# Two of four gate tokens as a high and a low rounded product in the PEER gate stage

## The chip, the cores and the metric

The kernel runs on one core of one Trainium2 chip. The metric is the device time of one launch in microseconds (us). Of three runs of the kernel before, the median is 3161.97 us, the lowest 3159.41 us and the highest 3166.76 us. One further execution was profiled; every row below is from it.

## The reference, cut to what matters

The kernel computes one layer of a hybrid decoder on 1024 prompt tokens and 32 sample tokens, width 1024: a mixer (gated linear attention and S5) and then PEER, a layer of 16384 single-neuron experts of which each token uses 128. Only PEER matters here:

```python
def peer_ffn(h, w_query, sub_keys, expert_u, expert_v):
    ...
    gate = jax.nn.softmax(fin_s, axis=-1)
    idx = fin_i.reshape(T, PEER_HEADS * PEER_TOPK)
    ...
        act = jax.nn.gelu(jnp.einsum('tkd,td->tk', expert_u[ik], xk))
        return jnp.einsum('tk,tkd->td', gk * act, expert_v[ik])
```

An expert's number is `i * 128 + j`, with `i` and `j` from two lists of 128 keys. All arrays are float32. A float32 product on TensorE is one instruction of the program and two records in the trace; a product of two operands of the rounded type (`F32R`, float32 with the low mantissa bits rounded away, written fp32r where VectorE or ScalarE makes it) is one record.

## The kernel before, in words

704 of the tokens are treated densely: for them the kernel computes the activations of all 16384 experts, and multiplies them with a dense matrix of gates that is zero where a token doesn't use the expert. The other 352 tokens fetch rows of single experts by indirect DMA.

The gates stage (`peer_gates`) builds that matrix of gates. For each token it needs a 128x128 matrix W[j, i] that holds the token's 128 gates at their places. It is a product over the 128 selections: `hot_j` (selection x j, one where the selection's j is this one) is the stationary operand, `hot_i` (selection x i, the selection's gate where its i is this one, else zero) the moving one. Tokens go in groups of four (`BT`), 176 groups (`BANKS`). For each group VectorE makes `hot_j` in one instruction of 512 elements (L2478) and `hot_i` in four of 128 (L2483, `one_hots`), TensorE makes four float32 products of 128 columns into one PSUM bank (L2525), and ScalarE copies the bank out (L2546) to a buffer of 64 tokens, which SyncE writes to memory (`w_d`) when it is full.

The stage runs through 192 steps (`STEPS`), three for each of the last 64 of the 128 expert blocks. Beside the groups, each engine does its part of the expert activations (`Up`): TensorE makes in step kind 0 the first and in kind 2 the second half of a block's activations (L1894, 24 products of 352 columns of the rounded type each), in kind 1 it turns the next rows of `peer_u` (L1884, 8 transposes). ScalarE applies gelu (L1909) in kinds 0 and 2, and rounds the turned rows (L1902) in kind 1; VectorE makes the low part of them (L1914). VectorE also does the row work of the 352 sparse tokens (L1948, L1956) on rows that GpSimd fetches (L1941). Each step has then one group (two in two of the steps), as `groups_at` says. The order on each engine is the order in which the code is written; semaphores connect them:

- `hot` counts groups made by VectorE; TensorE waits for it before a group. `made` counts groups of TensorE; VectorE keeps at most three groups (`NHB`) ahead by it, and ScalarE waits for it before a copy.
- `stored` counts ScalarE's copies; TensorE waits before group g for the copy of group g - 2.
- gelu waits until the DMA of the same half of the previous block (`kept`) has landed. Those DMAs, the loads of `peer_u` and the writes of `w_d` share SyncE's queue.

## Time and profile before

| | us |
|---|---|
| median of three runs | 3161.97 |
| lowest, highest | 3159.41, 3166.76 |
| profiled execution, its own time | 3162.19 |
| its span, first to last instruction | 3160.5 |
| granted TensorE clock over the span | 0.988 |
| the gates stage, first to last group | 656.6 |

In the rows, PE is TensorE's matmul side, PEld its loads of the stationary operand, DVE VectorE, ACT ScalarE, POOL GpSimd, SP SyncE. The type of an operand of TensorE is printed as f32 whether it is float32 or rounded. A group's row gives the busy time of all its instructions together and the mean duration of one; on TensorE these durations overlap, so that the distance from one start to the next is shorter than a duration. The number after a bar is the idle time of the engine just before these instructions, and what ended it.

### The profile page before, as it was taken

How to read it: one execution, taken by the hardware profiler on the slowest of the kernel's cores; microseconds unless marked ns; L12 is line 12 of the kernel's file. 1: busy time of each engine (PE TensorE's matmuls, PEld its weight loads, DVE VectorE, ACT ScalarE, POOL GpSimd, SP SyncE). 2: the span in 40 equal slices, each digit the busy share in tenths (PEclk: the TensorE clock that was granted, in tenths of full speed). 3: DMA queues.
4: the chain of work that ended last, by engine and by line, in shares of the span. 5: the costliest groups of instructions: out<-in, count | busy, mean ns of one | idle time of the engine just before them, and what ended most of it. 6: DMA issues, size and time to landing. Idle time of an engine off the chain costs nothing. (4 is left out here: it accounts for less than half of the span.)

```text
span 3160.5 us, 45816 instructions
## 1 busy us (share of the span) xinstructions
PE 3098.8 (98%) x17420; PEld 2727.1 (86%) x17420; DVE 2510.0 (79%) x5568; ACT 882.8 (28%) x1308; POOL 929.2 (29%) x758
## 2 busy tenths in 40 slices
PE   8999989989999999999999999998999999999999
PEld 7867765489999999999999999997888888888887
DVE  6621244366889999998999999976999999999997
ACT  4210210132122222223444444432222222222222
POOL 0000000000022323323334334333554544444451
PEclk9999989989999999999999999999999999999999
DMA  3010021261167777777998898999999999999994
GB/s 105 15 42 29 14 87 47 78 190 52 54 219 243 248 243 245 246 244 239 322 349 307 330 347 309 328 339 360 357 352 336 335 351 331 336 352 340 333 339 158
DMA packets 359906, 754.88 MB, mean 239 GB/s; under 512 B 37084, under 2 KB 205880, under 8 KB 354040
## 3 DMA queue, kind: packets, MB, share of 16 engines
q0 software_dynamic: 102576, 373.47, 34.8%
q1 hardware_dynamic: 257112, 378.49, 34.2%
q8 instruction: 139, 2.28, 0.3%
q14 instruction: 79, 0.65, 0.1%
HBM read 647.21 MB, written 102.25 MB: 237 GB/s over the span
## 5 line engine op out<-in xcount | busy, mean ns | idle before, releaser
L1941 POOL DMA_INDIRECT lead<-in_peer_v_dram,chosen x190 | 276.1, 1453 | 285.7 <-DVE xs L1956 253.7
L1941 POOL DMA_INDIRECT gr_row<-in_peer_u_dram,chosen x205 | 240.3, 1172 | 346.1 <-DVE chosen L1948 273.1
L1909 ACT ACTIVATE up_a<-up_pa 128x352 f32<-128x352 f32 x256 | 118.8, 464 | 756.7 <-PE up_pa L1894 684.5
L1948 DVE CUSTOM_DVE_ANT_0 gr_row<-gr_row,xs 128x1024 f32<-128x1024 f32 x205 | 248.6, 1221 | 35.3 <-DMA gr_row<-in_peer_u_dram,chosen 33.7
L1941 POOL DMA_INDIRECT s_sb<-in_peer_u_dram,chosen x147 | 158.9, 1081 | 375.5 <-DVE chosen L1948 369.9
L1956 DVE SCALAR_TENSOR_TENSOR xs<-lead,chosen,xs 128x1024 f32<-128x1024 f32 x190 | 243.4, 1281 | 11.8 <-DMA xs<-x_d 4.0
L1941 POOL DMA_INDIRECT dr_row<-in_peer_v_dram,chosen x126 | 179.6, 1425 | 192.9 <-DVE xs L1956 173.8
L511 PE MATMUL fr_a<-pj_w,h_t 128*128 128x256 f32 (+1 forms) x864 | 198.4, 392 | 0.9 <-PEq L186 0.9
L2483 DVE TENSOR_SCALAR pg_hot_i<-pg_iota,sel_t 128x128 f32<-128x128 f32 x704 | 195.8, 358 | 0.0
L511 PEld LDWEIGHTS fr_a<-pj_w,h_t 128*128 128x128 f32 (+1 forms) x864 | 170.1, 226 | 28.2 <-issue 6.4
L2525 PE MATMUL pg_pw<-pg_hot_i,pg_hot_j 128*128 128x128 f32 x1408 | 185.9, 275 | 2.4 <-DVE pg_hot_i L2483 2.4
L2525 PEld LDWEIGHTS pg_pw<-pg_hot_i,pg_hot_j 128*128 128x128 f32 x1408 | 176.5, 192 | 2.6 <-DVE pg_hot_i L2483 2.6
L1948 DVE CUSTOM_DVE_ANT_0 s_sb<-s_sb,xs 128x1024 f32<-128x1024 f32 x147 | 178.7, 1216 | 0.0
L2347 ACT ACTIVATE lo_wx<-room 128x704 fp32r<-128x704 f32 x128 | 101.0, 789 | 273.9 <-DVE room L2338 249.8
L1956 DVE SCALAR_TENSOR_TENSOR xs<-dr_row,chosen,xs 128x1024 f32<-128x1024 f32 x126 | 161.5, 1282 | 4.7 <-DMA dr_row<-in_peer_v_dram,chosen 0.6
L2752 DVE TENSOR_TENSOR acc<-pd_po,acc 128x512 f32<-128x512 f32 x200 | 128.5, 683 | 8.4 <-PE pd_po L2833 8.2
L1884 PE MATMUL up_pt<-up_ident,lead 128*128 128x128 f32 x1024 | 132.5, 272 | 1.3 <-PEq L1464 1.3
L2478 DVE TENSOR_TENSOR pg_hot_j<-pg_iota,sel_t 128x512 f32<-128x512 f32 x176 | 121.4, 690 | 14.9 <-PE pg_pw L2525 14.7
L1894 PE MATMUL up_pa<-h_dh,up_ut1h 128*128 128x352 f32 x688 | 130.7, 332 | 2.1 <-PEq L71 2.1
L1894 PE MATMUL up_pa<-h_dh,up_ut0h 128*128 128x352 f32 x688 | 129.3, 330 | 0.7 <-DVE up_ut0l L1914 0.7
L1894 PE MATMUL up_pa<-h_dh,up_ut2h 128*128 128x352 f32 x672 | 127.1, 331 | 0.0
L1894 PE MATMUL up_pa<-h_dh,up_ut1l 128*128 128x352 f32 x688 | 124.6, 323 | 0.0
(521 smaller groups left out, 7503.4 us busy)
## 6 DMA issues: line engine op xcount, KB each, us to landing
lead<-in_peer_u_dram SPq DMA_DIRECT2D x128, 512.0 KB
room<-in_peer_v_dram SPq DMA_DIRECT2D x128, 512.0 KB
act_d<-up_a SPq DMA_DIRECT2D x256, 176.0 KB
room<-w_d SPq DMA_DIRECT2D x64, 704.0 KB
room<-act_d SPq DMA_DIRECT2D x64, 704.0 KB
w_d<-pg_wb SPq DMA_DIRECT2D x24, 1024.0 KB, 8.9
w_d<-room SPq DMA_DIRECT2D x20, 1024.0 KB
lead<-in_peer_wq_dram SPq DMA_DIRECT2D x20, 512.0 KB
```

The lines of the kernel that those rows point to most:

```text
L511: mm = nc.tensor.matmul(out, h_t[:, k, tok], w[piece % 2][:, k, :], start=(k == 0), stop=(k == KD - 1))
L1884: mm = self.nc.tensor.transpose(self.turn_bank(n, half)[:, k * P:(k + 1) * P], self.u_sb[n % self.NU_IN][:, c:c + P], self.ident[:])
L1894: mm = self.nc.tensor.matmul(self.pa[c][:, 0:WB], self.ut[n % self.NB][x][:, k, :], self.h[y][:, k, c * WB:(c + 1) * WB], start=(i == 0), ...
L1909: self.nc.scalar.activation(self.a_sb[c][:], self.pa[c][:, 0:WB], ACT.Gelu_apprx_tanh).then_inc(self.a_act, 1)
L1941: pool.indirect_dma_start(self.buf[i % self.n], None, table, bass.IndirectOffsetOnAxis(ap=self.idx[:, col:col + 1], axis=0)).then_inc(self ...
L1948: self.nc.vector.tensor_tensor_reduce(row, row, xs[:, slot_of(col), :], 1.0, 0.0, ALU.mult, ALU.add, raw[:, col:col + 1]).then_inc(self.us ...
L1956: self.nc.vector.scalar_tensor_tensor(out=out, in0=self.buf[i % self.n], scalar=w[:, col:col + 1], in1=out, op0=ALU.mult, op1=ALU.add).the ...
L2347: self.nc.scalar.activation(self.wx[m % RING][:, 0:TD].rearrange("j (c t) -> j c t", t=WCH), self.w[m // 2 % 2][:, :, m % 2], ACT.Copy).th ...
L2478: nc.vector.tensor_tensor(hot_j[:, hb], iota[:].unsqueeze(1).broadcast_to([P, BT, P]), sel_t[:, 1, g * BT:(g + 1) * BT].unsqueeze(2).broad ...
L2483: ins = nc.vector.tensor_scalar(hot_i[:, hb, j, :], iota[:], sel_t[:, 0, tok], sel_t[:, 2, tok], ALU.is_equal, ALU.mult)
L2525: mm = nc.tensor.matmul(pw[g % 2][:, j, :], hot_j[:, g % NHB, j, :], hot_i[:, g % NHB, j, :], start=True, stop=True)
L2752: nc.vector.tensor_tensor(out, banks[at % NBANKS][:], out, ALU.add).then_inc(emptied, 1)
```

## The change

Of a group's four tokens, the first two are treated as before. For the other two:

- VectorE writes the gate one-hot in the rounded type (`hot_h`, the gate's high part). `hot_j` is now of the rounded type for all four tokens; the first two read it as float32. A one or a zero is exact in it.
- ScalarE makes `hot_l`, the low part, as `hot_h` times a share per selection and token, the ratio of the gate's low part to its high part: two activations of 128 elements a group, with the share as a per-partition scale (`low_parts`). They are placed before the copy of the group ahead: the low parts of group g + 1 stand before the copy of group g.
- TensorE makes two products of the rounded type, with the same stationary operand: high, then low, added up in PSUM. Before the first of them it waits for `low`.
- Before the first group VectorE computes the shares of all 352 such tokens: a rounding copy, a maximum, a subtraction, a reciprocal and a multiplication over 352 elements, the subtraction and the multiplication in two pieces each (32 and 320).

The line numbers change: L2520 and L2526 (`one_hots`), L2568, L2573 and L2574 (the products), L2588 (the low parts), L2609 (the copy).

```diff
-            hot_i, hot_j = (hots.enter_context(nc.sbuf_tensor("pg_hot_" + x, [P, NHB, BT, P], F32, side="right")) for x in "ij")
+            def hot_room(name, shape, dt):
+            hot_i = hot_room("i", [P, NHB, BT // 2, P], F32)
+            hot_h = hot_room("h", [P, NHB, BT // 2, P], F32R)
+            hot_j = hot_room("j", [P, NHB, BT, P], F32R)
+            hot_l = hot_room("l", [P, 2, BT // 2, P], F32R)
+            shares = hot_room("shares", [P, BANKS * BT // 2 - FIRST_SHARES], F32)
...
+        rounded, shared, low = sem("rounded"), sem("shared"), sem("low")
+        pieces = [(0, FIRST_SHARES, raw[:, COLS - FIRST_SHARES:COLS]), (FIRST_SHARES, BANKS * BT // 2, shares[:])]
+        def share_of(n):
+            return raw[:, COLS - FIRST_SHARES + n:COLS - FIRST_SHARES + n + 1] if n < FIRST_SHARES else (
+                shares[:, n - FIRST_SHARES:n - FIRST_SHARES + 1])
...
+            n_split = BANKS * BT // 2
+            split = sel_t[:, 2, :].rearrange("p (g h b) -> p g h b", h=2, b=BT // 2)[:, :, 1, :]
+            high = hot_h[:].rearrange("p a b n -> p (a b n)")[:, 0:n_split]
+            part = hot_i[:].rearrange("p a b n -> p (a b n)")[:, 0:n_split]
...
+            nc.vector.tensor_copy(by_group(high), split).then_inc(rounded, 1)
+            dve.wait_ge(rounded, 1)
+            nc.vector.tensor_scalar(part, high.bitcast(F32), 1e-30, None, ALU.max).then_inc(rounded, 1)
+            for first, last, out in pieces:
+                ins = nc.vector.tensor_tensor(by_group(out), split[:, first * 2 // BT:last * 2 // BT],
+                                              by_group(high[:, first:last]).bitcast(F32), ALU.subtract)
+            ins.then_inc(rounded, 1)
+            dve.wait_ge(rounded, 3)
+            nc.vector.reciprocal(part, part).then_inc(rounded, 1)
+            dve.wait_ge(rounded, 4)
+            for first, last, out in pieces:
+                ins = nc.vector.tensor_tensor(out, out, part[:, first:last], ALU.mult)
+            ins.then_inc(shared, 1)
+            dve.wait_ge(shared, 1)
...
                 for j in range(BT):
                     tok = slice(g * BT + j, g * BT + j + 1)
-                    ins = nc.vector.tensor_scalar(hot_i[:, hb, j, :], iota[:], sel_t[:, 0, tok], sel_t[:, 2, tok],
+                    out = hot_h[:, hb, j - BT // 2, :] if j >= BT // 2 else hot_i[:, hb, j, :]
+                    ins = nc.vector.tensor_scalar(out, iota[:], sel_t[:, 0, tok], sel_t[:, 2, tok],
                                                   ALU.is_equal, ALU.mult)
                 ins.then_inc(hot, 1)
...
                     pe.wait_ge(hot, g + 1)
                     if g >= 2:
                         pe.wait_ge(stored, g - 1)
-                    for j in range(BT):
-                        mm = nc.tensor.matmul(pw[g % 2][:, j, :], hot_j[:, g % NHB, j, :], hot_i[:, g % NHB, j, :],
-                                              start=True, stop=True)
+                    for j in range(BT // 2):
+                        nc.tensor.matmul(pw[g % 2][:, j, :], hot_j[:, g % NHB, j, :].bitcast(F32), hot_i[:, g % NHB, j, :],
+                                         start=True, stop=True)
+                    pe.wait_ge(low, g + 1)
+                    for j in range(BT // 2, BT):
+                        one = hot_j[:, g % NHB, j, :]
+                        nc.tensor.matmul(pw[g % 2][:, j, :], one, hot_h[:, g % NHB, j - BT // 2, :], start=True, stop=False)
+                        mm = nc.tensor.matmul(pw[g % 2][:, j, :], one, hot_l[:, g % 2, j - BT // 2, :], start=False, stop=True)
                     mm.then_inc(made, 1)
...
+            def low_parts(g):
+                if g == 0:
+                    act.wait_ge(shared, 1)
+                act.wait_ge(hot, g + 1)
+                if g >= 2:
+                    act.wait_ge(made, g - 1)
+                for j in range(BT // 2):
+                    ins = nc.scalar.activation(hot_l[:, g % 2, j, :], hot_h[:, g % NHB, j, :].bitcast(F32), ACT.Copy,
+                                               scale=share_of(g * BT // 2 + j))
+                ins.then_inc(low, 1)
+            low_parts(0)
...
                 for g in groups_at(s):
+                    if g + 1 < BANKS:
+                        low_parts(g + 1)
                     c, t0 = g // BC, g % BC * BT
                     if c >= 2 and t0 == 0:
                         act.wait_ge(wrote[buffer_of(c)], 16 * PIECES * (c // 2))
```

TensorE's queue around a step of kind 1, before: one group, the transposes (`up_pt`), one group.

```order
L1894 MATMUL up_pa<-h_dh,up_ut0l 128x352 x8
L2525 MATMUL pg_pw<-pg_hot_i,pg_hot_j 128x128 x4
L1884 MATMUL up_pt<-up_ident,lead 128x128 x8
L2525 MATMUL pg_pw<-pg_hot_i,pg_hot_j 128x128 x4
L1894 MATMUL up_pa<-h_dh,up_ut0h 128x352 x8
```

And after:

```order
L1894 MATMUL up_pa<-h_dh,up_ut2l 128x352 x8
L2568 MATMUL pg_pw<-pg_hot_i,pg_hot_j 128x128 x2
L2573 MATMUL pg_pw<-pg_hot_h,pg_hot_j 128x128
L2574 MATMUL pg_pw<-pg_hot_l,pg_hot_j 128x128
L2573 MATMUL pg_pw<-pg_hot_h,pg_hot_j 128x128
L2574 MATMUL pg_pw<-pg_hot_l,pg_hot_j 128x128
L1884 MATMUL up_pt<-up_ident,lead 128x128 x8
```

Nothing moved past anything; four products a group became six, of which the last four need `hot_l`.

ScalarE's queue at the start of the stage, before: the gelu of the gates' selections, then gelu of `up_a`, the copy of group 0, the rounding of turned rows (`up_ut0h`), the copy of group 1.

```order
L2531 ACTIVATE chosen<-chosen 128x128
L1909 ACTIVATE up_a<-up_pa 128x352
L2546 ACTIVATE pg_wb<-pg_pw 128x4x128
L1902 ACTIVATE up_ut0h<-up_pt 128x512 x2
L2546 ACTIVATE pg_wb<-pg_pw 128x4x128
```

And after (`chosen` in the rows of `pg_hot_l` is the buffer `raw`, where the first 32 shares lie):

```order
L2588 ACTIVATE pg_hot_l<-pg_hot_h,chosen 128x128 x2
L1909 ACTIVATE up_a<-up_pa 128x352
L2588 ACTIVATE pg_hot_l<-pg_hot_h,chosen 128x128 x2
L2609 ACTIVATE pg_wb<-pg_pw 128x4x128
L1902 ACTIVATE up_ut0h<-up_pt 128x512 x2
L2588 ACTIVATE pg_hot_l<-pg_hot_h,chosen 128x128 x2
L2609 ACTIVATE pg_wb<-pg_pw 128x4x128
```

The low parts that TensorE needs in the next step stand behind this step's gelu or roundings, and ahead of this step's copy.

VectorE's queue at the start of the stage, after; before, L2471 (now L2489) was followed by the one-hots at once:

```order
L2489 TENSOR_TENSOR chosen<-chosen 128x128
L2501 CAST pg_hot_h<-sel_t 128x352
L2503 TENSOR_SCALAR pg_hot_i<-pg_hot_h 128x352
L2505 TENSOR_TENSOR chosen<-sel_t,pg_hot_h 128x32
L2505 TENSOR_TENSOR pg_hot_shares<-sel_t,pg_hot_h 128x320
L2509 RECIPROCAL pg_hot_i<-pg_hot_i 128x352
L2512 TENSOR_TENSOR chosen<-chosen,pg_hot_i 128x32
L2512 TENSOR_TENSOR pg_hot_shares<-pg_hot_shares,pg_hot_i 128x320
L2520 TENSOR_TENSOR pg_hot_j<-pg_iota,sel_t 128x512
```

Seven instructions now stand ahead of the first one-hots.

## Rows read from the trace of the kernel before

**Rows 1.** The page, busy time and share of the span, by engine.

```profile
PE 3098.8 (98%) x17420; PEld 2727.1 (86%) x17420; DVE 2510.0 (79%) x5568; ACT 882.8 (28%) x1308; POOL 929.2 (29%) x758
```

**Rows 2.** The gates stage: stretch, its length, busy us of each engine, clock, DMA share, GB/s.

```profile
1440.90:2097.50 656.60, 654.19 (x4660) 653.95 (x4659) 619.00 (x1410) 292.91 (x408) 265.21 (x225) 1.00 0.90 322
```

**Rows 3.** Groups of instructions of that stage: count, busy us and mean ns, idle before.

```profile
L2483 DVE TENSOR_SCALAR pg_hot_i<-pg_iota,sel_t 128x128 f32<-128x128 f32 x704 | 195.8, 358 | 0.0
L2525 PE MATMUL pg_pw<-pg_hot_i,pg_hot_j 128*128 128x128 f32 x1408 | 185.9, 275 | 2.4 <-DVE pg_hot_i L2483 2.4
L2478 DVE TENSOR_TENSOR pg_hot_j<-pg_iota,sel_t 128x512 f32<-128x512 f32 x176 | 121.4, 690 | 14.9 <-PE pg_pw L2525 14.7
```

**Rows 4.** Waits of that stage: total us, times, longest us.

```profile
ACT up_a L1909 <- DMA act_d<-up_a: 36.4, 10, 5.7
DVE gr_row L1948 <- DMA gr_row<-in_peer_u_dram,chosen: 18.4, 18, 3.2
```

**Rows 5.** Timeline around 1605 us: start, length of the merged run, count.

```profile
1604.41 1.45 PE L1894 MATMUL up_pa<-h_dh,up_ut0l 128*128 128x352 f32 x8
1605.70 1.05 PE L2525 MATMUL pg_pw<-pg_hot_i,pg_hot_j 128*128 128x128 f32 x8
1606.59 1.04 PE L1884 MATMUL up_pt<-up_ident,lead 128*128 128x128 f32 x8
```

**Rows 6.** Timeline, the first two loads after idle time: transposes, rounded, float32 product.

```profile
881.31 0.20 PEld L1884 LDWEIGHTS up_pt<-up_ident,lead 128*128 128x128 f32 x2 [1.54 <-issue]
1440.49 0.30 PEld L1894 LDWEIGHTS up_pa<-h_dh,up_ut1h 128*128 128x128 f32 x2 [2.31 <-issue]
1448.77 0.30 PEld L2525 LDWEIGHTS pg_pw<-pg_hot_i,pg_hot_j 128*128 128x128 f32 x2 [2.65 <-DVE pg_hot_i L2483]
```

**Rows 7.** Groups of loads in the stage: float32, rounded, transposes.

```profile
L2525 PEld LDWEIGHTS pg_pw<-pg_hot_i,pg_hot_j 128*128 128x128 f32 x1408 | 176.5, 192 | 2.6 <-DVE pg_hot_i L2483 2.6
L1894 PEld LDWEIGHTS up_pa<-h_dl,up_ut1h 128*128 128x128 f32 x320 | 52.3, 188 | 0.0
L1884 PEld LDWEIGHTS up_pt<-up_ident,lead 128*128 128x128 f32 x464 | 52.7, 141 | 0.0
```

**Rows 8.** Groups of ScalarE's instructions, whole span, by shape.

```profile
L2343 ACT ACTIVATE lo_vx5h<-room 128x1024 fp32r<-128x1024 f32 x16 | 17.0, 1060 | 25.9 <-DMA room<-in_peer_v_dram 14.2 <-PE pd_po L2833 11.7
L261 ACT ACTIVATE n_hn<-n_x,n_rstd 128x1024 f32<-128x1024 f32 x8 | 9.2, 1148 | 0.3
L2032 ACT ACTIVATE tk_choice<-tk_choice 128x128 f32<-128x128 f32 x7 | 2.2, 312 | 0.1
```

**Rows 9.** Timeline, two of the places where gelu came after a DMA.

```profile
1528.97 1.06 PE L2525 MATMUL pg_pw<-pg_hot_i,pg_hot_j 128*128 128x128 f32 x8
1529.10 0.46 ACT L1909 ACTIVATE up_a<-up_pa 128x352 f32<-128x352 f32 x1 [4.46 <-DMA act_d<-up_a]
2068.11 1.06 PE L2525 MATMUL pg_pw<-pg_hot_i,pg_hot_j 128*128 128x128 f32 x8
2069.46 0.47 ACT L1909 ACTIVATE up_a<-up_pa 128x352 f32<-128x352 f32 x1 [5.67 <-DMA act_d<-up_a]
```

**Rows 10.** Timeline, the start of the stage.

```profile
1441.51 1.11 DVE L2483 TENSOR_SCALAR pg_hot_i<-pg_iota,sel_t 128x128 f32<-128x128 f32 x4
1444.44 1.05 PE L2525 MATMUL pg_pw<-pg_hot_i,pg_hot_j 128*128 128x128 f32 x8
1445.86 1.22 DVE L1948 CUSTOM_DVE_ANT_0 gr_row<-gr_row,xs 128x1024 f32<-128x1024 f32 x1 [3.24 <-DMA gr_row<-in_peer_u_dram,chosen]
1448.78 1.76 PE L2525 MATMUL pg_pw<-pg_hot_i,pg_hot_j 128*128 128x128 f32 x8 [2.41 <-DVE pg_hot_i L2483]
```

**Rows 11.** Groups of VectorE's instructions, whole span, by shape.

```profile
L2358 DVE TENSOR_TENSOR lo_wx<-room,lo_wx 128x64 fp32r<-128x64 f32 x128 | 28.2, 220 | 0.0
L2170 DVE RECIPROCAL tk_choice<-tk_choice 128x8 f32<-128x8 f32 x7 | 1.4, 203 | 0.2
L299 DVE RECIPROCAL n_rinv<-n_ss 128x1 f32<-128x1 f32 x8 | 1.3, 164 | 0.3
```

More of the change, by code:

```diff
@@ L2290 @@
 PIECES = 4
+FIRST_SHARES = 32
 STEPS = 3 * UP_GATES
@@ L2399, in peer_gates @@
         with ExitStack() as hots:
-            hot_i, hot_j = (hots.enter_context(nc.sbuf_tensor("pg_hot_" + x, [P, NHB, BT, P], F32, side="right")) for x in "ij")
+            def hot_room(name, shape, dt):
+                return hots.enter_context(nc.sbuf_tensor("pg_hot_" + name, shape, dt, side="right"))
+            hot_i = hot_room("i", [P, NHB, BT // 2, P], F32)
[3 more added lines that the diff above has]
+            shares = hot_room("shares", [P, BANKS * BT // 2 - FIRST_SHARES], F32)
         lower.place_first(nc)
@@ L2472, in _, with by_group @@
             dve.wait_ge(shaped, 1)
+            n_split = BANKS * BT // 2
+            split = sel_t[:, 2, :].rearrange("p (g h b) -> p g h b", h=2, b=BT // 2)[:, :, 1, :]
+            high = hot_h[:].rearrange("p a b n -> p (a b n)")[:, 0:n_split]
+            part = hot_i[:].rearrange("p a b n -> p (a b n)")[:, 0:n_split]
+            def by_group(x):
+                return x.rearrange("p (g b) -> p g b", b=BT // 2)
+            nc.vector.tensor_copy(by_group(high), split).then_inc(rounded, 1)
[12 more added lines that the diff above has]
+            dve.wait_ge(shared, 1)
             def one_hots(g):
```

## The prediction, made before the changed kernel ran

> **What bounds the kernel now.** I read the page first: TensorE is busy 98% of the span [rows 1]. [...] So TensorE bounds the stage, and VectorE stands 37.6 us behind it. The third view, groups and waits, says how firm that distance is: of VectorE's idle time only 14.7 us is waiting for TensorE, that is, being far enough ahead; 18.4 us is waiting for fetched rows, which a faster TensorE would not give back [rows 3, 4]. The fourth view is the timeline of single steps, to get the distance from start to start, since TensorE's durations overlap [rows 5].
>
> **TensorE: the products.** A group's four float32 products are eight records, from 1605.70 to 1606.59, 111 ns each [rows 5]. The change keeps four of them (two tokens) and puts four rounded ones (two tokens, high and low) in place of the other four. So the number of records and of loads is the same, and the question is what a rounded record of 128 columns takes. [...]
>
> But each record has its own load of the stationary operand, and there is one load ahead at most: the next starts when its predecessor's product starts. After idle time, where no product covers it, the second load of a rounded product starts 0.30 - 0.19 = 0.11 us after the first, as it does for a float32 one; for a transpose it is 0.20 - 0.14 = 0.06 us [rows 6, 7]. The durations say the same: 188 ns for a rounded load, 192 for a float32 one, 141 for a transpose's [rows 7]. So a rounded load of 128 columns occupies the loader about 108 ns, as long as the float32 product it stands beside now. [...] I take 111 ns for the new records: 0 us saved. [...]
>
> [...]
>
> **ScalarE: the low parts.** Two activations of 128 elements with a per-partition scale. One without such a scale takes 312 ns; the scale adds 1148 - 1060 = 88 [rows 8]. So 2 x 0.40 = 0.8 us a group, 141 us in all; ScalarE goes from 293 to 434 of 656 us, off the path by its sum. It isn't by its order. TensorE needs the low parts of group g + 1 after the first two tokens of that group, and they stand behind the gelu of the step before. In a step of kind 0 the gelu starts about when the up products end. TensorE then has group g (0.89), the transposes (eight records too, 0.9) and two tokens (0.45) ahead, 2.2 us [rows 5], against 0.46 + 0.8 = 1.26 on ScalarE [rows 8, 9]: fits, with 1 us over. Before the groups of the other two kinds stand 24 x 0.161 = 3.9 us of up products. So ordinary steps cost nothing, and VectorE is at least two groups ahead, so that the waited-for `hot` is there.
>
> Where gelu waits for the landing of its DMA, the 1 us is gone. There are ten such waits, 36.4 us [rows 4], and a few of the same kind put down to issue. I compared for each group the ScalarE time with TensorE's: four are late. The last: gelu starts at 2069.46, so the low parts would be there at 2069.46 + 1.26 = 2070.7, and TensorE wants them at 2068.11 + 0.45 = 2068.6: 2.1 us. The first: 1529.10 + 1.26 against 1528.97 + 0.45 gives 0.9 [rows 9]. The two between, at 1652 and 1888 us, give 1.3 and 1.9 the same way. Sum +6 us. Before, these waits hit nobody, because the copy of a group is needed only two groups later. Ends: 0 (the DMAs land in time, or the stall moves them) and +12 (each late place also delays the next, or all ten are late). I take +5, since part of a stall gives the DMA queue time.
>
> **VectorE.** Its work per group is the same in number and size. The rounded output of two of four small instructions is not shown by any row of one source; two-source ones write it at the same speed, 220 ns for 64 elements and 690 for 512 without it, 1.05 ns an element [rows 3, 11]. I take no difference; the bound above is that 128 elements lose half their rate, 128 x 1.05 / 2 = 67 ns each, and below 0.
>
> Ahead of the first group come seven instructions. By 1.05 ns an element the two-source ones cost 0.49 (320) and 0.19 (32), twice: 1.36. The copy and the maximum lie between 0.28 (128 elements, 195.8 / 704) and 0.52 (352 of two sources): 0.4 each. The reciprocal: 164 ns for one element and 203 for eight is 5.6 ns an element, 2.1 us for 352 [rows 3, 11]. Sum 4.3; the bounds are 2.5, with the reciprocal at 1.05 ns an element too, and 4.5, with copy and maximum at 0.52. What it costs at the end: the first one-hots end at 1441.51 + 1.11 = 1442.6 now, and 1446.9 then; TensorE wants them at 1444.44 and finishes the first group, with the low parts, at about 1448.0 instead of 1445.3. But VectorE then idles 3.2 us for its first fetched row until 1445.86, and that goes: it starts it at 1446.9, 1.1 late [rows 10]. The second group, for which TensorE now waits 2.41 us, comes 1.1 us later and its low parts 0.8 after its one-hots, of which 0.45 lies beside its first two tokens: done at about 1451.0 instead of 1450.1. So +1 us. That rests on the idle time of 3.2 being cover; without it +4. A second stretch of half clock (one falls there now: the group after the wait takes 1.76 instead of 1.05) could add 1.5.
>
> **The sum**, against the profiled execution's 3162.2 us (span 3160.5), which lies 0.2 above the median of 3162.0: products 0, low parts +5, start +1, so 3168 us.
>
> **Rivals.**
> [...]
> 2. VectorE takes over the bound, the other side. If the rounded one-hots lose half their rate, 352 x 67 ns = 23.6 us come on VectorE: 619.0 + 4.3 + 23.6 + 19.4 of row waits = 666.3 against 656.6. It decides from 13.9 us of added work, 40 ns an instruction. +10, with the start 3173 us. For: nothing shows a one-source rounded output. [...] Against: two-source rounding costs nothing here.
> 3. The low parts are always in time: ScalarE's DMA waits fall elsewhere in another execution. 3163 us.
> [...]
>
> **Chances.** The forecast 0.44, rival 1 0.16, rival 2 0.12, rival 3 0.20, rival 4 0.08. A measurement of this kernel tells 0.2%, 6.3 us, from no change: below 3155.7 or above 3168.3. The forecast's case lies at that upper edge, so half of it (0.22) goes to each side. Faster 0.16 (rival 1), same 0.22 + 0.20 = 0.42, slower 0.22 + 0.12 + 0.08 = 0.42. Range 3150 to 3178: it leaves out part of rival 1 and of rival 4. The likeliest case alone has 3163 to 3175.
>
> **What would show it.** Right: the starts of the rounded products 108 to 113 ns apart, and a group from its first to its last start as long as now; TensorE idle before the high products with ScalarE's low parts as the releaser, 3 to 10 us in a few places, each behind a gelu that waited for a DMA; the two activations 0.8 us; VectorE's one-hots still 0.28 each; the first group about 2.7 us later and the second 1. Wrong: starts below 100 ns apart, or a VectorE with less than 5 us of waiting for TensorE and TensorE waiting for `hot`, or low parts late in many steps, which would mean that ScalarE's order costs far more than I read.

## The result, and where the time went

The changed kernel takes 3174.3 us (median of six runs, 3172.5 to 3180.6) against 3163.5 for the kernel before on the same chip: a ratio of 1.0035, 95% interval 1.0025 to 1.0045, so 11 us slower. 3168 was forecast. The time lies inside the range, but most of the difference comes from a place that the prediction didn't name.

The busy line of the page after, to be read against [rows 1]: TensorE has 13 us more, VectorE 4 and ScalarE 90.

```profile
PE 3112.0 (98%) x17420; PEld 2737.4 (86%) x17420; DVE 2513.9 (79%) x5575; ACT 972.5 (31%) x1660; POOL 923.8 (29%) x758
```

The profiled execution of after is the longest of its six (3180.6 us), and its stage began 4.0 us later than before's although no instruction ahead of it had changed. So I compare the stage alone, from its first up product to the end of its last group. This is its row, with the same columns as [rows 2]:

```profile
1444.51:2113.76 669.25, 663.58 (x4657) 662.10 (x4658) 623.47 (x1417) 382.50 (x760) 262.06 (x226) 1.00 0.88 316
```

In the kernel before it is 1440.52 to 2097.18, 656.7 us. The stage is 12.6 us longer, with TensorE busy for 9.4 us more (663.6 against 654.2) at the same clock of 1.00 in both rows. So most of it is not waiting. VectorE has 4.5 us more, the seven instructions of the start.

Its groups of instructions: the one-hots of both types, the high and the low products and ScalarE's low parts, against [rows 3] and [rows 7].

```profile
L2520 DVE TENSOR_TENSOR pg_hot_j<-pg_iota,sel_t 128x512 fp32r<-128x512 f32 x176 | 120.7, 686 | 28.1 <-PE pg_pw L2574 28.0
L2588 ACT ACTIVATE pg_hot_l<-pg_hot_h,pg_hot_shares 128x128 fp32r<-128x128 f32 x320 | 109.9, 396 | 0.0
L2526 DVE TENSOR_SCALAR pg_hot_i<-pg_iota,sel_t 128x128 f32<-128x128 f32 x352 | 104.8, 339 | 0.0
L2526 DVE TENSOR_SCALAR pg_hot_h<-pg_iota,sel_t 128x128 fp32r<-128x128 f32 x352 | 104.8, 365 | 0.0
L2573 PE MATMUL pg_pw<-pg_hot_h,pg_hot_j 128*128 128x128 f32 x352 | 93.5, 291 | 2.9 <-ACT pg_hot_l L2588 2.8
L2574 PEld LDWEIGHTS pg_pw<-pg_hot_l,pg_hot_j 128*128 128x128 f32 x352 | 67.6, 192 | 0.0
```

VectorE waits for TensorE 28.0 us, where it was 14.7 [rows 3]: TensorE has moved further from VectorE, not nearer. Both one-hot types have the same 104.8 us, and the load of a low product lasts 192 ns like that of a float32 one [rows 7].

The waits of the stage, against [rows 4]:

```profile
ACT up_a L1909 <- DMA act_d<-up_a: 24.4, 6, 5.3
...
PE pg_pw L2573 <- ACT pg_hot_l L2588: 2.8, 3, 1.6
```

TensorE waits for low parts for 2.8 us. So where are the other 10 us? The timeline of TensorE shows them. One turn of the loop (a block of three steps: transposes, group, second up half (step kind 2), group, first up half of the next block (kind 0), group), first of before, then of after. Columns are start, length of the merged run, and its records.

```profile
1505.67 1.04 PE L1884 MATMUL up_pt<-up_ident,lead 128*128 128x128 f32 x8
1506.55 1.06 PE L2525 MATMUL pg_pw<-pg_hot_i,pg_hot_j 128*128 128x128 f32 x8
1507.36 1.51 PE L1894 MATMUL up_pa<-h_dh,up_ut0h 128*128 128x352 f32 x8
1508.71 1.43 PE L1894 MATMUL up_pa<-h_dl,up_ut0h 128*128 128x352 f32 x8
1509.98 1.43 PE L1894 MATMUL up_pa<-h_dh,up_ut0l 128*128 128x352 f32 x8
1511.24 1.05 PE L2525 MATMUL pg_pw<-pg_hot_i,pg_hot_j 128*128 128x128 f32 x8
...
1516.89 1.04 PE L1884 MATMUL up_pt<-up_ident,lead 128*128 128x128 f32 x8
```

```profile
1601.48 1.06 PE L1884 MATMUL up_pt<-up_ident,lead 128*128 128x128 f32 x8
1602.38 0.61 PE L2568 MATMUL pg_pw<-pg_hot_i,pg_hot_j 128*128 128x128 f32 x4
...
1603.22 1.54 PE L1894 MATMUL up_pa<-h_dh,up_ut2h 128*128 128x352 f32 x8
1604.61 1.49 PE L1894 MATMUL up_pa<-h_dl,up_ut2h 128*128 128x352 f32 x8
1605.94 1.49 PE L1894 MATMUL up_pa<-h_dh,up_ut2l 128*128 128x352 f32 x8
1607.27 0.61 PE L2568 MATMUL pg_pw<-pg_hot_i,pg_hot_j 128*128 128x128 f32 x4
...
1608.11 1.50 PE L1894 MATMUL up_pa<-h_dh,up_ut0h 128*128 128x352 f32 x8
...
1612.00 0.61 PE L2568 MATMUL pg_pw<-pg_hot_i,pg_hot_j 128*128 128x128 f32 x4
...
1612.84 1.06 PE L1884 MATMUL up_pt<-up_ident,lead 128*128 128x128 f32 x8
```

The group's eight records take 1603.22 - 1602.38 = 0.84 us (1507.36 - 1506.55 = 0.81 before), and the loads of the high and low ones start 112 ns apart, as forecast. But the block takes 1612.84 - 1601.48 = 11.36 us, and 1516.89 - 1505.67 = 11.22 before (11.213 and 11.360 as the median over the stage's blocks). Each part counts from its first start to the first start of the next. Few of the 147 ns lie in the three groups: by the medians these have +15, the transposes +23, the second up half +162 and the first -53. The change touches none of the last three. The second half's 24 products take 1607.27 - 1603.22 = 4.05 us (8 in 1605.94 - 1604.61 = 1.33, 167 ns each) and took 1511.24 - 1507.36 = 3.88 (8 in 1.27, 159 ns). The first half went from 3.945 to 3.892 (1612.00 - 1608.11). Over 58.7 blocks (176 groups, three a block) 147 ns are 8.6 us. The same instructions on the same operands run at one of several paces, without a wait on the record: 3.885 or 4.047 us the second half, 3.945 or 3.892 the first, as medians of before and after.

### The profile page after: what moved, and what is told of

Read it like the earlier page. It is cut to its first block and busy times, and to the rows that moved or that the text cites. A ratio compares the mean times of both kernels' runs of the same rounds, so it can differ in the third digit from the quotient of the medians.

```text
span 3178.8 us, 46350 instructions
## 1 busy us (share of the span) xinstructions
PE 3112.0 (98%) x17420; PEld 2737.4 (86%) x17420; DVE 2513.9 (79%) x5575; ACT 972.5 (31%) x1660; POOL 923.8 (29%) x758
## 5 line engine op out<-in xcount | busy, mean ns | idle before, releaser
L2520 DVE TENSOR_TENSOR pg_hot_j<-pg_iota,sel_t 128x512 fp32r<-128x512 f32 x176 | 120.7, 686 | 28.1 <-PE pg_pw L2574 28.0
L1894 PE MATMUL up_pa<-h_dl,up_ut1h 128*128 128x352 f32 x688 | 125.6, 324 | 0.0
L1894 PE MATMUL up_pa<-h_dh,up_ut0l 128*128 128x352 f32 x688 | 125.4, 324 | 0.0
L1894 PE MATMUL up_pa<-h_dl,up_ut0h 128*128 128x352 f32 x688 | 125.3, 324 | 0.0
```

What stands on the lines that cost most here:

```text
L1894: mm = self.nc.tensor.matmul(self.pa[c][:, 0:WB], self.ut[n % self.NB][x][:, k, :], self.h[y][:, k, c * WB:(c + 1) * WB], start=(i == 0), ...
L2520: nc.vector.tensor_tensor(hot_j[:, hb], iota[:].unsqueeze(1).broadcast_to([P, BT, P]), sel_t[:, 1, g * BT:(g + 1) * BT].unsqueeze(2).broad ...
```

## The experiments

Three theories. A: the pace of the unchanged up products is set by the order and types of TensorE's own products, and is most of the loss. B: ScalarE's 352 more activations disturb TensorE. C: low parts that come late, and the start, are the loss. The table has what all kernels gave. "Stage" is the profiled stage, "halves" the second and the first up half, "block" the median of the blocks; a half or block counts from its first start to the first start of what follows. The us given with each experiment are the ratio less one, times the time of the kernel before on the same chip; where their range spans zero, the runs tell no difference. All products are as in the changed kernel where nothing is said.

| kernel | ratio to before, 95% | stage us | halves us | block us |
|---|---|---|---|---|
| before | 1 | 656.7 | 3.885, 3.945 | 11.213 |
| after | 1.0035 (1.0025 to 1.0045) | 669.3 | 4.047, 3.892 | 11.360 |
| 1 zero low operand | 1.0027 (1.0016 to 1.0038) | 665.0 | 4.047, 3.892 | 11.360 |
| 2 low parts early | 1.0024 (1.0014 to 1.0034) | 664.6 | 4.046, 3.893 | 11.360 |
| 3 waits, products as before | 1.0009 (1.0001 to 1.0018) | 659.2 | 3.885, 3.945 | 11.213 |
| 4 zero, rounded first | 0.9997 (0.9988 to 1.0006) | 656.7 | 3.883, 3.946 | 11.213 |
| 5 zero, high only | 0.9959 (0.9943 to 0.9974) | 640.0 | 3.87, 3.89 | 10.51, more with waits |
| 6 start only | 1.0005 (0.9996 to 1.0014) | 656.0 | 3.885, 3.945 | 11.213 |
| 7 rounded first, all work | 1.0007 (0.9998 to 1.0016) | 657.7 | 3.884, 3.946 | 11.213 |
| 8 rounded first before second half | 1.0011 (1.0002 to 1.0020) | 662.6 | 3.885 or 4.068, 3.91 or 3.89 | in turn |
| 9 zero, float32 first and last | 0.9996 (0.9987 to 1.0005) | 655.4 | 3.885, 3.926 | 11.193 |
| 10 the same, all work | 1.0003 (0.9994 to 1.0012) | 658.0 | 3.885, 3.926 | 11.193 |
| 11 zero, all but second half | 1.0033 (1.0019 to 1.0046) | 668.2 | 4.048, 3.949 | 11.413 |
| 12 zero, rounded at both ends | 1.0028 (1.0016 to 1.0039) | 664.8 | 4.049, 3.892 | 11.360 |

**1. Zero low operand.** ScalarE fills it once with zeros; no shares, no low parts.

```diff
-                    pe.wait_ge(low, g + 1)
+                    if g == 0:
+                        pe.wait_ge(low, 1)
-                    ins = nc.scalar.activation(hot_l[:, g % 2, j, :], hot_h[...], ACT.Copy, scale=share_of(...))
+                    ins = nc.scalar.activation(hot_l[:, b, j, :], iota[:], ACT.Copy, scale=0.0)
```

> The changed kernel without the low parts' work: the low operand is a buffer of zeros that ScalarE fills once, so the output lacks the low parts; VectorE makes no shares, ScalarE no low parts, and TensorE waits for them once. Its eight products of a group stay as they are. Theory A (the pace of TensorE's unchanged up products after a group is set by how the run is entered, so by the products in front of it): a block of three steps still takes 11.36 us against 11.21 before, 58 of them +8.5 us, the up run after a group 4.05 us; time +8 to +9 us over the kernel before. Theory B (ScalarE's 352 more activations disturb TensorE's operand reads): a block falls back to 11.21 us, time within 1 us of the kernel before. Theory C (the whole loss is low parts that come late, and the start): within 1 us of the kernel before too.

+8.5 us (5.1 to 12.0). ScalarE is back at 293.9 us of work, no low part is ever late, and the block is still 11.36 us:

```profile
1446.28:2111.23 664.95, 662.62 (x4657) 662.38 (x4658) 619.44 (x1410) 293.87 (x412) 263.25 (x226) 1.00 0.89 318
```

B and C fall as the main cause. TensorE's own products cost 8.3 us of stage (664.95 against 656.7). The trace also shows that a record does not slow down by what ScalarE or GpSimd does beside it: in the second halves of 1 a record takes 166.7 ns on average where ScalarE is busy all through it (345 records) and where it is idle (755), and the same holds for GpSimd (309 and 774). VectorE is busy beside nearly all of them, so that this says nothing of it. Nor do the zeros matter: the kernels with the real low parts have the same blocks as those with zeros (2 as 1, 7 as 4, 10 as 9).

**2. Low parts early.**

```diff
+                ahead = [g + 1 for g in groups_at(s) if g + 1 < BANKS]
+                if ahead:
+                    low_parts(ahead[0])
                 if k == 0:
                     up.gelu(act, n, 0)
```

> The changed kernel with ScalarE making a group's low parts ahead of the gelus and roundings of the step instead of behind them, so that a gelu which waits for its DMA no longer holds them up. Theory C (late low parts are the loss): 5 to 10 us less than the changed kernel, so +1 to +6 over the kernel before. Theory A (pace): only the three later waits (0.8, 1.0 and 1.85 us) and the half-clock stretch behind the last (1.6 us) go, 3 to 5 us less than the changed kernel, so +6 to +8 over the kernel before, with a block still at 11.36 us. A loss instead would mean that the low parts, which must wait for VectorE's one-hots and for a buffer, hold up the gelus.

+7.6 us (4.4 to 10.8), 3.5 less than after (the difference of two ratios, so give or take 4 to 5). All three later waits for low parts are gone and the block stays at 11.36. A's number; C explains the 4.7 us between the two stages, and no more.

**3. Waits, products as before.** Four float32 products; the low parts are made, waited for and not used.

```diff
-                        nc.tensor.matmul(..., one, hot_h[...], start=True, stop=False)
-                        mm = nc.tensor.matmul(..., one, hot_l[...], start=False, stop=True)
+                        mm = nc.tensor.matmul(..., hot_j[...].bitcast(F32), hot_h[...].bitcast(F32), start=True, stop=True)
```

> Everything of the change on VectorE and ScalarE and TensorE's wait for the low parts, but TensorE's four products of a group all float32 as before (the low parts are made and not used). Theory A: a block returns to 11.21 us; what is left is the waits and the start, +3 to +7 us over the kernel before. Theory B: a block stays at 11.36 us and the time near the changed kernel's, +10 to +14. If the chips' pace is set by the waits on the low parts themselves, also 11.36 us.

```profile
1441.83:2101.07 659.24, 654.31 (x4658) 653.02 (x4658) 623.35 (x1416) 382.60 (x760) 266.68 (x226) 1.00 0.90 321
```

+2.8 us (0.3 to 5.7), just under A's +3 to +7. With ScalarE's 382.6 us of work and all waits TensorE's busy time is before's 654.3: B falls altogether. 1 and 3 together (8.5 + 2.8) make up after's 11.

**4. Zero, rounded first.**

```diff
+                    for j in range(BT // 2, BT):  (the high and low products)
+                        ...
+                    for j in range(BT // 2):      (the float32 products)
+                        ...
-                    for j in range(BT // 2):      (float32)
-                    for j in range(BT // 2, BT):  (high and low)
```

> The kernel with the zero low operand (no low parts made, output without them), and in each group the four rounded products ahead of the two float32 ones, so that a float32 product is again the last before the up run. Theory A in its narrow form (the last products before the run set its pace): the up run after a group returns to 3.89 us and the block to 11.21 us, time within 1 us of the kernel before. In its wide form (any rounded product in the group shifts the entry): the block keeps another value than 11.21 us, and stays near the kernel with zeros and the old order, +8 us. Theory B and C: within 1 us of the kernel before.

-0.9 us (-3.8 to +1.9). The block is before's to the nanosecond (11.213), and both halves are within 2 ns. The same eight records in another order take 8.3 us less in the stage than in 1. This is what A in its narrow form says, a float32 product last; 5, 8, 9, 11 and 12 bear on that further. It also shows that four rounded records cost what four records of float32 products cost.

**5. Zero, high only.** The low products are left out.

```diff
-                        mm = nc.tensor.matmul(..., one, hot_l[...], start=False, stop=True)
```

> The kernel with the zero low operand, but without the products of the low parts (output without them): a group has six records instead of eight. What one rounded record is worth: if it is paced by the 108-ns load of its own stationary operand, the two that go are worth 111 ns each, 0.22 us in each of 176 groups, -39 us at most; VectorE, which needs 619 us of the stage's 657 before, then becomes the bound after -34 us or less, with waits of TensorE for the one-hots. [...] If TensorE's work in the stage is set by something else, no change.

```profile
PE pg_pw L2545 <- DVE pg_hot_h L2503: 16.3, 17, 2.8
```

-13 us (-18 to -8). A group of six records takes 0.616 us where eight took 0.840: 112 ns for each record taken away, against the 108 that the prediction read from their load. TensorE then waits for one-hots 17 times, 16.3 us: VectorE is the bound, at 16.7 us under the stage before instead of the 34 that I had put as the limit. Left out of the 34 are VectorE's waits for fetched rows, which the prediction had counted (19.4 us in rival 2): its work of 612.3 us and 26.6 us of such waits are 638.9 of the stage's 640.0.

The second half is a surprise. Here is one of a block without waits, its first start and the start of the group behind it:

```profile
1471.55 1.49 PE L1894 MATMUL up_pa<-h_dh,up_ut0h 128*128 128x352 f32 x8
...
1475.42 0.60 PE L2545 MATMUL pg_pw<-pg_hot_i,pg_hot_j 128*128 128x128 f32 x4
```

Each group of 5 ends with a rounded product, as in the changed kernel, and its six records stand as far apart as the first six of after's eight within 2 ns. Yet the half takes 1475.42 - 1471.55 = 3.87 us, not 4.05. Of the 57 second halves 49 took 3.85 to 3.87 us and three 4.05; of the other five, four have a wait in them and one half clock. So a rounded product last in front does not give the slow pace by itself.

**6. Start only.** The shares on VectorE, and float32 products; no low parts on ScalarE.

> Only the shares that VectorE works out at the stage's start, and the rounded type of two of four one-hots; TensorE's products all float32 as before, and ScalarE makes no low parts. If the start is the term of +1 us of the prediction: within 2 us of the kernel before, the first group 2.5 us later and the second 0 to 1 us. A theory of a costly start (the 4.3 us on VectorE stay on the path) gives +3 to +4 us. A block of 11.21 us in both.

The seven instructions and what follows them on TensorE:

```profile
1443.94 0.34 DVE L2501 CAST pg_hot_h<-sel_t 128x352 fp32r<-128x352 f32 x1
...
1448.20 0.69 DVE L2520 TENSOR_TENSOR pg_hot_j<-pg_iota,sel_t 128x512 fp32r<-128x512 f32 x1
...
1449.98 0.71 PE L2568 MATMUL pg_pw<-pg_hot_i,pg_hot_j 128*128 128x128 f32 x4 [2.32 <-DVE pg_hot_h L2526]
...
1452.75 0.71 PE L2568 MATMUL pg_pw<-pg_hot_i,pg_hot_j 128*128 128x128 f32 x4 [0.74 <-DVE pg_hot_h L2526]
```

1448.20 - 1443.94 = 4.26 us for the seven (4.3 forecast). The first group starts 6.42 us after the stage instead of 3.92, 2.5 later. But the stage is 0.7 us shorter than before's (655.99), in the runs +1.6 us (-1.3 to +4.4). The clock row of before tells why. In the kernel before, the second wait [rows 10] is followed by a stretch at 0.50 of the clock; in this kernel 4 us there are at 1.00 (first row before, second row this kernel).

```profile
1449.20:1450.90 1.70, 1.70 (x9) 1.70 (x8) 1.70 (x6) 0.33 (x1) 0.77 (x1) 0.50 1.01 403
```

```profile
1449.00:1453.00 4.00, 2.28 (x18) 2.04 (x19) 4.00 (x12) 1.83 (x3) 1.15 (x1) 1.00 0.95 336
```

The start of after, 2 and 3 has no such stretch either. In 7, 8 and 10, where TensorE waits for the low parts earlier in a group, the clock is at 0.50 for 3.4, 6.8 and 6.8 us there, and in the six kernels without shares for 3.4 us, as in the kernel before.

**9. Zero, float32 first and last.**

```diff
+                    for j in (0, 2, 3, 1):
```

> The kernel with the zero low operand (no low parts), and a group's products in the order float32, rounded, rounded, float32: the group begins as in the changed kernel and ends as in the kernel before. If the last product alone sets the pace of the run behind it: 3.89 and 3.94 us for the two up runs, a block at 11.21 us, time within 2 us of the kernel before. If the first product, or the place of the rounded ones in the group, sets it: the run after the turn keeps 4.05 us, a block 11.36 us, +8 us.

-1.3 us (-4.1 to +1.6), block 11.193. With a float32 product last, what stands first doesn't matter to the second half (3.885 us), and makes 20 ns in the first.

**8. Rounded first only in front of the second half.** All the work, early low parts.

```diff
+                    if k == 1:
+                        (rounded, then float32)
+                    else:
+                        (float32, then rounded, as in the changed kernel)
```

> The changed kernel with all its work, ScalarE's low parts ahead of the step's gelus, and the rounded products ahead of the float32 ones in one group in three only: the one in front of the second up half, whose run took 167 ns a record. Theory A (the last product in front of a run sets its pace): that run returns from 4.05 to 3.89 us, the run in front of which nothing is changed stays at 3.89 us, a block takes 11.16 to 11.21 us; time within 2 us of the kernel before, 8 to 10 us under the same kernel with the old order. If the pace hangs on all of a block's groups together: a block between 11.21 and 11.36 us. A wait for the low parts, which now stands at the head of every group, adds up to 2 us where they are late.

Here my narrow form fell. The second half in two blocks that follow each other:

```profile
1604.71 0.66 PE L2574 MATMUL pg_pw<-pg_hot_i,pg_hot_j 128*128 128x128 f32 x4
1605.13 1.51 PE L1894 MATMUL up_pa<-h_dh,up_ut2h 128*128 128x352 f32 x8
1606.48 1.43 PE L1894 MATMUL up_pa<-h_dl,up_ut2h 128*128 128x352 f32 x8
1607.75 1.43 PE L1894 MATMUL up_pa<-h_dh,up_ut2l 128*128 128x352 f32 x8
...
1615.90 0.66 PE L2574 MATMUL pg_pw<-pg_hot_i,pg_hot_j 128*128 128x128 f32 x4
1616.32 1.56 PE L1894 MATMUL up_pa<-h_dh,up_ut0h 128*128 128x352 f32 x8
1617.72 1.49 PE L1894 MATMUL up_pa<-h_dl,up_ut0h 128*128 128x352 f32 x8
1619.06 1.50 PE L1894 MATMUL up_pa<-h_dh,up_ut0l 128*128 128x352 f32 x8
```

The same float32 products stand in front of both (the run begins 0.42 us after the first of them each time), and 8 up products take 1.27 us in one block and 1.34 in the next, in turn through the whole stage. The time, +3.5 us (0.6 to 6.3), lies between the orders, not within 2 us. So a float32 product last isn't enough. The low parts and the wait for them at a group's head are not what makes it alternate: 7 has both, and every block alike.

**11. The reverse of 8: only the group in front of the second half as in the changed kernel, with zeros.**

```diff
+                    if k != 1:
+                        (rounded, then float32)
+                    else:
+                        (float32, then rounded)
```

> The kernel with the zero low operand (no low parts), rounded products first in two groups of three (in front of the transposes and of the first up half), and the changed kernel's order only in the group in front of the second up half. If what stands directly in front of a run sets its pace: the second half keeps 4.05 us, the first half goes to 3.95 us, a block at 11.36 us or more. If the pace is carried on through a whole block: the second half leaves 4.05 us though nothing directly in front of it was changed (3.88 to 3.95 us, a block near 11.2 us), or takes two values in turn.

```profile
1610.40 0.27 PE L2561 MATMUL pg_pw<-pg_hot_l,pg_hot_j 128*128 128x128 f32 x1
1610.52 1.54 PE L1894 MATMUL up_pa<-h_dh,up_ut0h 128*128 128x352 f32 x8
1611.90 1.50 PE L1894 MATMUL up_pa<-h_dl,up_ut0h 128*128 128x352 f32 x8
```

+10.4 us (6.0 to 14.6), every second half behind the start at 4.05 us. So with eight records a group, what stands directly in front does decide in one direction: with a rounded product last there, the second half takes 4.05 us in the steady loop of after, 1, 2 and 11. With six records it does not (5). With float32 last it takes 3.88 in before, 3, 4, 6 and 9, but only in every other block of 8, where the group in front of the first half ends rounded. What 8 carries from block to block stays open: the buffers of a group's parity change from block to block as well, and no run tells these apart.

After 8 and 9 the theory had to be wider. A2: the pace is a state of the whole loop, which the order of the products in all groups sets, whatever ScalarE does beside it.

**7 and 10. The orders of 4 and 9 with all the work.** Experiment 10 has the order float32, rounded, rounded, float32; 7 all rounded first, with the wait for the low parts at the group's head. Both have 2's early low parts. The edit of 10:

```diff
-                    for j in range(BT // 2):
+                    for j in (0, 2, 3, 1):
+                        if j == BT // 2:
+                            pe.wait_ge(low, g + 1)
```

> The changed kernel with all its work, ScalarE's low parts ahead of the step's gelus, and the rounded products ahead of the float32 ones in every group. Theory A2 (the pace is a state of the whole loop that the order of the products in all groups sets, whatever ScalarE does beside it): every block at 11.21 us as with the zero low operand in this order, and time within 3 us of the kernel before (up to 3 us where the low parts of the first group, now waited for at its head, come late). Theory B (ScalarE's work beside it sets the pace): the blocks keep 11.35 us, +7 to +10 us.

> The changed kernel with all its work, ScalarE's low parts ahead of the step's gelus, and a group's products in the order float32, rounded, rounded, float32, so that TensorE waits for the low parts after the first product only. Theory A2: a block at 11.19 us as with the zero low operand, 1.2 us less than before over the stage, no late low parts behind gelus, start within 1 us: -2 to +1 us against the kernel before, 9 to 12 us under the changed kernel. Theory B: +7 to +10 us.

+2.2 us (-0.6 to +5.1) and +0.9 us (-1.9 to +3.8), with blocks of 11.213 and 11.193 in every turn but those at the start. As A2 has it: all of the change's work, and no slow half. 10 is some 10 us faster than the changed kernel, 3.5 of which the early low parts gave alone in 2, and level with the kernel before; nothing tried with the full computation beats that one. Its stage is 1.3 us longer than before's in spite of a shorter block (58 times 0.02 us), so the start cost 2.5 us and not the 1 us that I had expected, since its first groups wait for one-hots and low parts and the clock falls to half for 6.8 us there.

**12. Zero, rounded at both ends.** The order rounded, float32, float32, rounded.

```diff
-                    for j in (0, 2, 3, 1):
+                    for j in (2, 0, 1, 3):
```

> The kernel with the zero low operand (no low parts), and a group's products in the order rounded, float32, float32, rounded: its end is the changed kernel's, its inside and its begin are not. If a rounded product last in front of the second half is enough: that half takes 4.05 us in every block, a block about 11.36 to 11.41 us, +8 to +11 us over the kernel before. If the time from start to start inside the group decides (the changed kernel's second half took 3.86 us once where its group had been 14 ns longer): the second half takes another value, 3.86 to 3.95 us, or several in turn, a block between 11.17 and 11.3 us, -2 to +5 us.

+8.9 us (5.1 to 12.3). The second half took 3.86 us in one early block, and from the next one on 4.049 in all, a block 11.360. So with another inside and the changed kernel's end the loop is in the slow pace again. But the pace is not fixed by that end alone, as 5 has shown and as two odd places show. In after, the group at 1659 us is 14 ns longer than its neighbours (1660.04 - 1659.18 = 0.86 us instead of 1603.22 - 1602.38 = 0.84), and behind it eight up products take 1.27 us instead of 1.33:

```profile
1659.18 0.61 PE L2568 MATMUL pg_pw<-pg_hot_i,pg_hot_j 128*128 128x128 f32 x4
...
1660.04 1.48 PE L1894 MATMUL up_pa<-h_dh,up_ut1h 128*128 128x352 f32 x8
1661.36 1.43 PE L1894 MATMUL up_pa<-h_dl,up_ut1h 128*128 128x352 f32 x8
1662.62 1.43 PE L1894 MATMUL up_pa<-h_dh,up_ut1l 128*128 128x352 f32 x8
```

In experiment 3, with float32 products all through, one group is held up 51 ns (0.86 us instead of 0.81), and the second half behind it falls into the slow pace, this once:

```profile
2071.73 0.61 PE L2568 MATMUL pg_pw<-pg_hot_i,pg_hot_j 128*128 128x128 f32 x4
2072.17 0.66 PE L2572 MATMUL pg_pw<-pg_hot_h,pg_hot_j 128*128 128x128 f32 x4
2072.59 1.56 PE L1894 MATMUL up_pa<-h_dh,up_ut2h 128*128 128x352 f32 x8
2073.99 1.50 PE L1894 MATMUL up_pa<-h_dl,up_ut2h 128*128 128x352 f32 x8
```

So much is shown: the order and number of a group's products set the pace of the steady loop. That the pace hangs on the moment at which a run is entered, as A has it, is not shown. For it stand the two places above. Against it stand two places of after, where a group 0.38 us longer, at 1453.7 us, is followed by 4.05 us as usual, and a group of the usual 0.84 us, at 1910.7 us, by 3.86; in 8 two paces follow starts that agree within 2 ns; and in 5 the slow pace stays away. What carries the pace stays open.

## Why the prediction was right, and where it was not

**The products, 0 us: right by its own step.** A rounded record of 128 columns costs 112 ns beside its load (5), and eight mixed records cost what the eight records of four float32 products do (4: the same block of 11.213 us). That a load starts with the product ahead of its own can be read off the kernel before: the group's first load starts at 1605.55 us, and the last up product at 1604.41 + 7 x 0.161 = 1605.54 [rows 5]; of 4780 loads from 1460 to 2090 us 4387 start 1 to 4 ns after a product.

```profile
1604.26 1.32 PEld L1894 LDWEIGHTS up_pa<-h_dh,up_ut0l 128*128 128x128 f32 x8
1605.55 1.02 PEld L2525 LDWEIGHTS pg_pw<-pg_hot_i,pg_hot_j 128*128 128x128 f32 x8
```

Rival 1 of the chances is a rounded record that costs less than its load, rival 4 one that costs more. Both are out. For more columns than 128 a rounded record does take less than one of a float32 product. From start to start and at 512 columns these are (2702.66 - 2699.94) / 12 = 227 ns and (501.74 - 499.16) / 6 = 430 in the kernel before:

```profile
2699.94 0.62 PE L2833 MATMUL pd_po<-lo_vx5h,lo_wx 128*128 128x512 f32 x2
...
2702.66 0.39 PE L2833 MATMUL up_pa<-lo_vx3h,lo_wx 128*128 128x512 f32 x1
```

```profile
499.16 2.74 PE L1137 MATMUL gl_mo<-gl_w,zone_o_b 128*128 128x512 f32 x6
501.74 0.27 PE L1176 MATMUL gl_op<-zone_v,gl_prob 128*128 128x128 f32 x1
```

A rounded record of 352 columns takes 161 ns [rows 5], so a column (227 - 161) / 160 = 0.41 ns, and 128 columns would be 161 - 224 x 0.41 = 69 ns. That is an estimate from these rows, and what rival 1 could hope for. No run has it: 112 ns is what such a record takes with a load of its own.

**ScalarE's low parts, +5 us: right in its cause, in its size partly by luck.** Stage after less stage of 1, with 6's start taken off: 669.3 - 665.0 + 0.7 = 5.0 us. Experiment 2, which only moves the low parts, gives 669.3 - 664.6 = 4.7 us. They come late as forecast, behind a gelu that waited for its DMA. The last of the three places:

```profile
2082.02 0.46 ACT L1909 ACTIVATE up_a<-up_pa 128x352 f32<-128x352 f32 x1 [5.32 <-DMA act_d<-up_a]
2082.38 0.68 ACT L2588 ACTIVATE pg_hot_l<-pg_hot_h,pg_hot_shares 128x128 fp32r<-128x128 f32 x2
...
2083.11 0.33 PE L2573 MATMUL pg_pw<-pg_hot_h,pg_hot_j 128*128 128x128 f32 x1 [1.58 <-ACT pg_hot_l L2588]
```

The gaps there are 0.8, 1.0 and 1.8 us where 0.9, 1.3, 1.9 and 2.1 were forecast: 3.6 instead of 6, with one place fewer (ScalarE waited for this DMA 6 times, and 10 times before). The sum is met by something else that the term did not hold: behind the last one the clock is at 0.50 for 3.4 us, and the up half there takes 2089.08 - 2083.61 = 5.47 us instead of 4.05, 1.4 us more (1.6 is what I had put for it before experiment 2). The first fence is that stretch, the second is where the half and the next group start:

```profile
2084.70:2088.10 3.40, 3.40 (x14) 3.40 (x13) 3.40 (x8) 1.78 (x4) 0.92 (x1) 0.50 0.81 289
```

```profile
2083.61 1.74 PE L1894 MATMUL up_pa<-h_dh,up_ut2h 128*128 128x352 f32 x8
...
2089.08 0.61 PE L2568 MATMUL pg_pw<-pg_hot_i,pg_hot_j 128*128 128x128 f32 x4
```

The work itself was priced too high, at no cost to the forecast. An activation lasts 396 ns, as said (0.40), but two of them overlap and take 0.68 us, not 0.8; ScalarE has 90 us more and not 141.

**The start, +1 us: too dear by 1.7.** The work was 4.26 us as forecast, the first group 2.5 us late (2.7 forecast) and the second 0.9 (1). But the half-clock stretch of before was not repeated, which gave back more than the groups lost: 6 has -0.7. I had priced a second such stretch and not that the first would go.

**VectorE: right.** A rounded one-hot costs what a float32 one does (104.8 us for 352 of each; all 704 take 195.1 us together, and took 195.8), rival 2 is out, and so is rival 3, as the low parts were late.

**What the sum lacked: +8.3 us of pace.** The step that failed is the first one, which carried over the up products' time unchanged: "the number of records and of loads is the same" held for the group, and I had asked of the group only how far its own records stand apart. The order and type of the records moved the 24 unchanged products of the second half from 159 to 167 ns each, and shortened the first half by 53 ns. Experiment 1 has it by itself, and 4 takes it away with the same records. Terms that were measured: products 0, low parts +5.0, start -0.7, pace +8.3, which is the 12.6 us of the profiled stage; 11 us in the medians. That these add up proves nothing, as the 5.0 is what the other two leave of the 12.6; 2's 4.7 and the gaps with the clock, 3.6 + 1.4 = 5.0, are the readings that do not rest on them.

**The time is in the range by luck.** +6 us were forecast and 11 came. The named terms gave 4.3 us of stage together, and twice as much came from a term that the sum did not hold. The range reached to 3178 for later low parts and for rival 4, and down to 3150 for rival 1. No run shows a record that costs more or less than its load: 4 has before's block of 11.213 us, and 5 has 112 ns a record. The low parts weren't later than forecast either (3.6 us of gaps instead of 6). By the number alone, 3174.3, rival 2 (3173) would have passed for the cause; its own sign, slower one-hots, shows that it was not.

## What to carry to other kernels

When TensorE bounds a loop, compare the starts of its unchanged runs too, not only those of the edited products: a change of the types in front of a long run cost 4% of that run here with no wait in the profile (3.885 to 4.047 us), while another run became 1% shorter. If such a run slows, try another order of the same products first; here it gave back all of it in the steady loop (4 and 9 against 1, 7 and 10 against 2), for 1 to 2.5 us at the start where the low parts are real (7 and 10). Split a float32 product into rounded parts only if that lowers the number of records: at 128 columns, each with its own load, a rounded record costs here what a record of a float32 product costs (112 ns in 5, and the same block of 11.213 us in 4).

## What the runs showed of the hardware beyond that

- The same 24 products of 352 columns took 3.885, 3.892, 3.926, 3.945 or 4.047 us at a clock of 1.00, each value steady over some 50 blocks; with six records in a group the second half took 3.867 us. A single disturbance does not move the loop to another value for good: in after, the second halves behind three groups that were late or lengthened took 3.855 us, one in the block behind such a one 3.859, and those between them 4.047 again.
- A loop can alternate between two values, block by block (8: 3.885 and 4.068), while the starts in front of the run agree within 2 ns.
- A stretch of 3.4 us at a clock of 0.50 follows some waits of 1.6 to 2.4 us of TensorE and not others of the same length: it follows the 2.41-us wait in the kernel before [rows 10] and the 1.58-us one at 2083 us in after, and not the 2.32-us one at the start of 6. Which of them it follows is not worked out from these runs.
